# Four cache pages requested earlier and a later start for the gate tables, in a hybrid decoder step with a product-key expert layer

## What is computed

```
proj            = x @ w_in + b_in                      # q, k, v, gates of both mixers
y_a             = mLSTM(proj)                          # 4 heads, chunkwise scan, state C (128 x 256 per head)
kc, vc          = compress(K, V pages of the cache, 64-row blocks)   # learned linear compressor
o_cmp, o_slc    = attention over compressed blocks, and over selected blocks
o_win           = sliding-window attention
merged          = sigmoid(x @ w_merge) gates of (y_a @ w_br_a) and (y_b @ w_br_b)
h               = layer_norm(alpha * x + merged @ w_out)
# expert layer: 8 heads, 16384 experts = 128 x 128 product keys, top 16 per head
s1, i1 = top_k(q1 . keys1, 16);  s2, i2 = top_k(q2 . keys2, 16)
top_s, e = top_k(s1[:, None] + s2[None, :], 16);  gate = softmax(top_s)
out = sum over chosen e of gate * gelu(h . u[e]) * v[e]
y   = layer_norm(alpha * h + out)
```

## Time and profile before

| | |
|---|---|
| median of 3 runs | 2337.76 us (2336.2 to 2347.15) |
| the profiled execution | 2340.59 us |
| its span | 2338.9 us |
| mean granted TensorE clock | 0.961 |
| TensorE, VectorE, ScalarE, GpSimd busy | 94%, 64%, 42%, 39% |
| compression stage | 514 to 541 us |
| chunks of the expert stage | 1099 to 1785 us |
| second part of the expert stage | 1785 to 2330 us |

### The profile page before, as it was taken

How to read it: one execution, slowest core, us unless ns; L and a number is a source line. 1 busy time by engine, 2 the same in 40 slices (tenths; PEclk the granted TensorE clock), 3 DMA queues, 4 the chain that set the end, 5 groups by cost and what they waited for, 6 DMA issues and landing times.

```text
span 2338.9 us, 33988 instructions
## 1 busy us (share of the span) xinstructions
PE 2203.8 (94%) x13222; PEld 1922.2 (82%) x13222; DVE 1489.5 (64%) x3064; ACT 975.7 (42%) x1711; POOL 921.2 (39%) x605
## 2 busy tenths in 40 slices
PE   7999999977998999899987998999999999999998
PEld 7798987766556895599987998999998787888886
DVE  3234223344774343268899879966727888898986
ACT  2122222223884220133324664666645454445452
POOL 1001232311110000135866675768756555554530
PEclk9999999987997799999999998999999999999999
DMA  5243423345001152423887997989998999999993
GB/s 201 75 139 107 131 82 108 125 181 145 3 1 37 60 198 72 149 63 119 295 283 224 319 308 229 326 304 376 345 330 315 393 394 377 382 391 386 392 364 131
DMA packets 190232, 518.03 MB, mean 221 GB/s; under 512 B 15684, under 2 KB 85432, under 8 KB 185336
## 3 DMA queue, kind: packets, MB, share of 16 engines
q1 hardware_dynamic: 138648, 330.28, 40.1%
q0 software_dynamic: 50848, 184.53, 21.6%
q10 hardware_dynamic: 576, 1.05, 0.1%
HBM read 446.18 MB, written 73.75 MB: 222 GB/s over the span
## 4 chain that ended last, share of the span: by engine, by line
PE 45%; DVE 8%; DMA 3%; ACT 1%; issue 1%; POOL 0%; SPq 0%; DVEq 0%
PE ps_e L2348 21%; PE ps_e L2323 5%; PE ps_e L2319 5%; PE ps_e L2320 5%; PE ps_e L2340 3%; DMA u_raw<-in_peer_uT 2%; DVE row L2666 2%; PE ps_e L2371 2%; PE ps_e L2376 1%; PE ps_e L2377 1%; PE ps_e L2380 1%; PE ps_e L2308 1%; DMA e_gate<-gate_tables 1%; DVE oh L2607 0%; ACT one_b L2430 0%
## 5 line engine op out<-in xcount | busy, mean ns | idle before, releaser
L2270 POOL TENSOR_TENSOR u_lo<-u_raw,u_hi 128x1024 fp32r<-128x1024 f32 x128 | 316.4, 2473 | 108.1 <-ACT u_hi L2417 105.8
L2319 PE MATMUL ps_e<-hTh,u_hi 128*128 128x384 f32 x1024 | 357.2, 349 | 1.8 <-ACT gelu_out L2423 1.8
L2263 POOL DMA_INDIRECT row<-in_peer_v,sparse_idx x160 | 272.3, 1702 | 214.8 <-DVE y L2674 160.5
L2320 PE MATMUL ps_e<-hTl,u_hi 128*128 128x384 f32 x1024 | 349.1, 341 | 0.0
L2348 PE MATMUL ps_e<-v_hi,w_hi 128*128 128x512 f32 x768 | 243.4, 398 | 4.2 <-DVE v_lo L2694 2.8
L2348 PE MATMUL ps_e<-v_lo,w_hi 128*128 128x512 f32 x768 | 241.1, 395 | 0.0
L2348 PE MATMUL ps_e<-v_hi,w_lo 128*128 128x512 f32 x768 | 241.0, 395 | 0.0
L2694 DVE TENSOR_TENSOR v_lo<-v_raw,v_hi 128x1024 fp32r<-128x1024 f32 x128 | 161.9, 1266 | 95.5 <-ACT v_hi L2456 93.9
L2323 PE MATMUL ps_e<-hTh,u_lo 128*128 128x384 f32 x1024 | 202.9, 340 | 12.9 <-POOL u_lo L2270 12.9
L2319 PEld LDWEIGHTS ps_e<-hTh,u_hi 128*128 128x128 f32 x1024 | 196.1, 191 | 2.1 <-ACT u_hi L2417 2.1
L2263 POOL DMA_INDIRECT row<-in_peer_u,sparse_idx x150 | 156.8, 1046 | 101.4 <-DVE sparse_hid L2666 77.6
(11 more groups left out here) (509 smaller groups left out, 4712.7 us busy)
## 6 DMA issues: line engine op xcount, KB each, us to landing
u_raw<-in_peer_uT SPq DMA_DIRECT2D x128, 512.0 KB
v_raw<-in_peer_v SPq DMA_DIRECT2D x32, 2048.0 KB, 10.5
hidden_gelu<-gelu_out SPq DMA_DIRECT2D x64, 384.0 KB
gate_tables<-g_buf SPq DMA_DIRECT2D x48, 512.0 KB
e_gate<-gate_tables SPq DMA_DIRECT2D x32, 768.0 KB
gelu_in<-hidden_gelu SPq DMA_DIRECT2D x32, 768.0 KB
w_raw<-in_w_tiles SPq DMA_DIRECT2D x45, 512.0 KB, 3.6
gw_raw<-in_merge_tiles SPq DMA_DIRECT2D x16, 512.0 KB, 4.2
```

The costliest lines, as they stand in the source:

```text
L2263: pool.indirect_dma_start(out=row[:, :], out_offset=None, in_=io.peer_u if i < U_END else io.peer_v, in_offset=bass.IndirectOffsetOnAxis(a ...
L2270: pool.tensor_tensor(u_lo[:, n % UB, :, :], u_raw[:, n % UB, :, :], u_hi[:, n % UB, :, :].bitcast(F32), ALU.subtract).then_inc(ul_done, 1)
L2319: pe.matmul(ps[:, n % 2, 0:TD], u_hi[:, n % UB, dc, :], hTh[:, dc, :], start=(dc == 0), stop=False)
L2320: pe.matmul(ps[:, n % 2, 0:TD], u_hi[:, n % UB, dc, :], hTl[:, dc, :], start=False, stop=False)
```

## The change

Three things are done. SP asks for pages 0 to 3 behind filling tile 13 and no longer behind the compressor weights; pages 4 to 7 stay where they are. In the expert stage DVE uses 31 rows in place of 37 ahead of its loop, POOL gathers one row in place of two behind `low(14)` to `low(23)` and one each behind `low(24)` to `low(27)`, and the loop, the first turn and the first quads come two chunks later (28 to 30, 30 to 32), the second turn one later (57 to 58), the third where it was (85). The quads are spread over 82 in place of 84 chunks. The rows still to be done are spread as 68 over chunks 30 to 82 (before 65 over 28 to 82) and 61 over 82 to 118 (before 58).

```diff
@@ stage_mlstm, block.sync
                 if n in (6, 10):
                     load_c(2 if n == 6 else 3)
+                if n == 13:
+                    sp.wait_ge(c_sent[0], 32)
+                    for i in range(4):
+                        pg = sp.value_load(s.cmp_table[0:1, i:i + 1], min_val=0, max_val=io.cache_cmp_T.shape[0] - 1)
+                        src = io.cache_cmp_T[bass.ds(pg, 1)].rearrange("o p kv x -> (o p) (kv x)")
+                        sp.dma_start(s.cmp_xs[:, i, :, :, :].rearrange("p kv l x -> p (kv l x)"), src).then_inc(s.page_in, 16)
             sp.dma_start(s.bqT[:, :, :], io.bq_rows).then_inc(bq_in, 16)
             for kv in range(2):
                 sp.dma_start(s.cmp_w[:, kv, :, :], io.w_cmp[kv]).then_inc(s.cw_in[kv], 16)
-            for i in range(8):
-                if i % 4 == 0:
-                    sp.wait_ge(c_sent[i // 4], 32)
+            sp.wait_ge(c_sent[1], 32)
+            for i in range(4, 8):
                 pg = sp.value_load(...)
@@ stage_peer
-    E_AT, R_AT = (27, 56, 84), (28, 57, 85)
+    E_AT, R_AT = (29, 57, 84), (30, 58, 85)
...
-    quad_at = [30 + q * 84 // NQD for q in range(NQD)]
-    PRE = 37
+    quad_at = [32 + q * 82 // NQD for q in range(NQD)]
+    PRE = 31
     ROW_LEAD = 2
-    EARLY_AT = {n: 1 for n in (2, 3, 4, 5, 6, 8, 9, 11, 12, 13)} | {n: 2 for n in range(14, 24)}
+    EARLY_AT = {n: 1 for n in (2, 3, 4, 5, 6, 8, 9, 11, 12, 13)} | {n: 1 for n in range(14, 28)}
     assert sum(EARLY_AT.values()) + 7 == PRE
-    row_due = ([0] * PRE + [28 + i * 54 / 65 for i in range(65)]
-               + [82 + i * 36 / (U_END - PRE - 65) for i in range(U_END - PRE - 65)]
+    row_due = ([0] * PRE + [30 + i * 52 / 68 for i in range(68)]
+               + [82 + i * 36 / (U_END - PRE - 68) for i in range(U_END - PRE - 68)]
@@ stage_peer, block.vector, the list ahead of the loop
             rank(3, 0)
             rows(3)
             choose(HC, 0, HC)
-            rows(4)
+            rows(2)
             resolve(HC, 0, HC)
             below_top(0, PH)
-            rows(4)
             shares(0, 3, PH, gsp[:, 0:NS3].rearrange("p (h k) -> p h k", h=PH))
```

## The result

The kernel after takes 2324.26 us in the median of 7 runs (2321.76 to 2330.89), the kernel before 2337.76 (7 runs, 2336.2 to 2347.15): a ratio of 0.9936, 95% interval 0.9916 to 0.9957. Measured again among the experiments it is 2326.18 and 0.9943 (0.9924 to 0.9961). The change saves 13 to 15 us. The profiled execution has a span of 2322.2 us, 16.7 less than that of before, and TensorE's share of the chain is again 45%, as in the earlier trace rows.

A forecast was written before the change was run, and what follows sets the result against it. TensorE holds most of the chain, with DVE the bound around the first turn. Gains of 2.8 and 18 less losses of 2 and 4.6 give 14.2 us off the median 2337.8, so 2323.6; range 2312 to 2336.

The forecast's parts named there:

- Step 1: Compression stage: four pages asked for earlier let the last page land 2.8 us sooner; bounds 0 and 4.6.
- Rival D: Compression stage: the pages bring nothing, 2.8 us less gained, 2326; inside the forecast, whose 0.60 holds with or without it.
- Step 2: Expert stage up to the first turn: fewer early rows, single gathers and later turn win 18 us; bounds 9 and 22.
- Rival B: Ahead of the loop: DVE stops 5 us, not 2, per landing row; turn at 1242, time 2333; chance 0.14.
- Step 3: Expert loop, chunks 30 to 82: denser rows on DVE lose 2 us, turns hold; bounds 0 and 6.
- stay over the same critical chunks: Inside the loop: packed rows, 1.21 to 3.62 us each, move from chunks 50 to 76 to chunks 55 to 79.
- Step 4: Behind chunk 82: 61 rows for 58 on full DMA cost 4.6 us; bounds 0 and 9.
- The 8.8 us: Rows moved back into later chunks: by the skill's bandwidth rule all six paid in full, 8.8 us in place of 4.6.
- A: Later chunks: DMA gives back 9 us, not 4.6, and the denser middle costs DVE 6, not 2; 2332; chance 0.18.
- C: Packed-row chunks: DVE reductions colliding with POOL's low parts add up to 30 us; with 28, 2352; chance 0.04.
- The signs named for a wrong forecast: DVE waits over 15 us for rows ahead of the loop, no idle time at an exponential, or longer behind 1785.

The follow-up runs named there:

- pages only: Kernel before with only the four pages asked for earlier, expert stage as before: 2333.55 us, ratio 0.9969.
- its repeat: The kernel after, unchanged, measured and profiled once more against the kernel before: 2326.18 us, ratio 0.9943.
- expert part only: Kernel before with only the expert stage changed, pages asked for as before: 2329.24 us, ratio 0.9953.
- packed late: Kernel after with the reductions of the 32 packed rows moved from rows 64 to 95 to rows 100 to 131: 2312.92 us, ratio 0.9883.
- PSUM tokens: Kernel after with every reduced row reading the token's copy in PSUM, so packed rows' sums are wrong: 2312.57 us, ratio 0.9874.
- before with packed late: Kernel before with only the 32 packed rows moved from rows 64 to 95 to rows 100 to 131: 2334.67 us, ratio 0.9971.
- rows only: Kernel before with 31 rows ahead, mostly single gathers, 68 rows over chunks 28 to 82; turns, quads, pages as before: 2327.97 us, ratio 0.9941.
- shift only: Kernel before with only loop, turns and quads later; 37 rows ahead, paired gathers and pages as before: 2339.46 us, ratio 1.0000.

## Why the prediction was right, and where not

The time was forecast at 2323.6 and came at 2324.3; 13.4 us were saved where the sum said 14.2. By its own steps:

*Step 1, pages: right.* Taken 2.8; in the means the hole is 2.5 us smaller and the stage 2.9 shorter. The forecast put the hole at about 1.8 us; it is 2.7, since it was 5.2 and not 4.57 in most executions of before. Rival D is out. The time of pages only hints at more.

*Step 2, ahead of the loop: the size right, and half of the reasons.* Taken 18; at chunk 35 the four profiles of the expert part of after (after, its repeat, expert part only, packed late) are 15.8, 19.5, 16.8 and 16.6 us ahead of before, and PSUM tokens, the same up to there, is 19.1; before itself wanders by 2 to 3 us there (pages only, before with packed late). The waits for u_lo went, though POOL's gathers still waited 12.2 us for DVE, for 21.4, where the forecast had "little"; the turn came at 1235.1 on before's clock (1223.19 + 11.93) for 1233.5 forecast, and DVE stopped 6.5 us for rows between 1160 and 1250 where I took 6. Rival B is out. But the weight was misplaced: the single gathers and the two chunks of shift were credited with part of the 18, and neither shows in the time by itself. What is left for it are the six rows.

*Step 3, inside the loop: the step that failed.* Loss taken 2, bounds 0 and 6; from chunk 35 to 82 the same kernels (without packed late) lose 11.1, 11.5 and 13.4 against before, which itself wanders by 1.2 (pages only). The largest stop of TensorE in the stretch, behind the second turn, grew from 5.02 to 9.07 us (9.10 in the repeat and in expert part only), where the forecast said that the turns hold. The term counted DVE's extra rows by their number. What I wrote off as rows that "stay over the same critical chunks" is the largest single price that was measured in the stretch. With the packed rows out of it the kernel after stands 13 to 15 us earlier at chunk 82 (437.96 to 423.29 and 424.57), that of before 4.8 (442.70 to 437.93, the latter starting the stretch 3 us late, so 7.8 from chunk 35 on). So the packed rows cost TensorE some 8 us before and 10 to 14 after: a few us of the loss are this interaction, and without the packed rows the stretch is still 5 to 9 us longer after than before (259.2 and 263.0 for 254.3). The times say the same less sharply: with the packed rows late the change is worth 0.9883 / 0.9971 = 0.9912, 21 us, and 13 to 15 with them where they were, though the intervals (about 6 us each way for the first) touch. The rest is not pinned to one cause: DVE sets the pace there, in before as well, and a lead that TensorE wins at the first turn shrinks when it waits for DVE again. That the row count by chunk 82 fixes it has been tried and is wrong. The forecast of DVE's idle time, some 5 us, was met (5.90 and 6.64), and still the stop of 4.64 us came, some 20 us ahead of the second of them: a positive idle time at one point does not show that the chunks ahead of it have slack.

*Step 4, the last stretch: too dear, and a gain beside it that the sum did not have.* Taken 4.6. From chunk 82 to 127 the kernel after gains 0.4 us on before, its repeat 3.0, expert part only loses 2.6, and pages only, with before's transfers, loses 2.1. That is the sum of two things. From chunk 82 to 88, around the third turn, the three kernels need 31.9 us each and before 35.5 (pages only 36.5): 3.6 us won, of which the sum says nothing and whose cause stays open (rows only with 32.6 and shift only with 32.0 have most of it as well). From 88 to 127 they lose 3.2, 0.6 and 6.2 us. Over more profiles that stretch takes 203.6 us in the mean of four with 58 rows behind chunk 82, 206.0 in seven with 61, and 211.6 in two with 65. So the three rows cost some 2.4 us, half of the term, while the seven with 61 alone spread over 6 us. The sign named for it, ACT's waits for u_raw growing by 4 to 5 us, did not come: from chunk 82 to 127 they are 27.6 us before, 24.2 after, 19.9 in the repeat, and 30.9 in expert part only against 30.6 in pages only. The stretch still had some room at a share of 0.95; four rows more on top cost 6 to 8 us, about the 6 us that their 2.1 MB take at 352 GB/s. The 8.8 us that the prediction worked out by the Trainium skill's "SBUF — State Buffer", section "A bandwidth-pool intuition that's wrong (but worth ruling out)", are farther off still. The two terms that were off, -2 for some -11 and -4.6 for about 0 (3.6 and -3.2 in the first pair), do not cancel. The rest of the agreement comes from the stages ahead of chunk 0. The 16.7 us between the two spans are 11.9 ahead of chunk 0, 15.8 up to chunk 35, -11.1 to chunk 82, 0.4 to chunk 127 and -0.4 behind it. In the means the first of them is smaller: the mean start of chunk 0 is 1099.4 in the five profiles with before's pages and 1094.2 in the nine with after's, 5.2 for the 2.8 of step 1. That the sum hit the time to 1 us is partly luck. The spread that the prediction names, 2313 to 2329, is also narrower than its own bounds: with the first turn at 14 to 22 and the other terms at their bounds the sum runs from -1 to 27 us, so from 2311 to 2339.

*The rivals.* A ended too high, though its half on the denser middle (6 us for 2) was nearer to the 11 that were lost; its half on DMA was wrong for this change and right one step further. C, a collision more per chunk, named the right mechanism: the mean of a packed row was already 2.0 us before (64.8 us for 32, and the median of 1264 ns in the earlier trace rows hid it), so it went no further than to 68.7. It was priced as a danger, when it was an existing cost. That it is drawn anew with each shift in time, as the prediction says, fits the 60.3 to 79.1 us that the same 32 rows take in the kernels here. The signs named for a wrong forecast did not come, but for a trace of one: the part behind chunk 127, at 1784 before, is 0.4 us longer, 555.1 for 554.7. Pages only, with the expert part of before, has 557.1 there, so that is spread.

## What to carry to other kernels

Read the mean and the maximum of a group beside its median: 32 operations with a median of 1.26 us held 26 us of waiting. Where DVE paces the matmuls, take operands of long DVE operations from PSUM while POOL works in SBUF, or put the operations that can't be where DVE has room; here the second brought as much again as the change (2312.9 us, 0.9883), with not one instruction fewer. And price a time won ahead of a stretch that another engine paces only at what that stretch lets through: test it with one kernel per part, since the part that seems to win (the shift) may be worth nothing.

## What the runs showed of the hardware

What DMA moves in a stretch that looks full is not a fixed ceiling: the page of the kernel after has slices of 384 to 395 GB/s from 1800 us on, above the 341 GB/s of the stretch that I took for full, the 352 of the same stretch after, and the 371 of the earlier trace rows. What I took for full at 341 GB/s still took three more rows for some 2.4 us, where 1.57 MB at that rate are 4.6.

```profile
GB/s 202 77 134 109 126 94 109 127 183 146 2 2 38 88 171 77 145 74 136 271 304 232 336 301 251 299 319 358 371 336 308 386 388 384 387 393 384 395 354 131
```

The Trainium skill's page "SBUF — State Buffer", section "A bandwidth-pool intuition that's wrong (but worth ruling out)", gives about 358 GB/s for the path from HBM; these slices are 7 to 10% above it.

The same chunks, in kernels that have the same code there, reached chunk 82 between 442.7 and 445.8 us behind chunk 0 (before and pages only), and between 434.7 and 439.2 (after, its repeat and expert part only). Differences of 3 to 5 us in one stage of one pair of profiles are not evidence here; the holes of the compression stage, which repeat within 1 us in 14 profiles, are.
